# Feed-forward chunks 1 to 9 with the weight tile as stationary operand and the rows' two parts side by side

## The reference, cut to what matters

```python
def swiglu(h, w_gate, w_up, w_down):
    return (jax.nn.silu(h @ w_gate) * (h @ w_up)) @ w_down
# h: (256, 1024) float32, an rms_norm of x; w_gate, w_up: (1024, 2816); w_down: (2816, 1024)
# rmsnorm(x, g) = x * rsqrt(mean(x * x) + eps) * g
```

## Time and profile before

| | |
|---|---|
| median of 3 runs | 1907.35 us |
| lowest, highest | 1907.06, 1907.66 us |
| span of the profiled execution (first to last instruction) | 1904.2 us |
| the profiled execution's own time | not given apart; the median is 3.15 us over the span |
| PE, PEld busy | 98%, 80% |
| DVE, ACT, POOL busy | 58%, 50%, 8% |
| DMA moved | 332.72 MB, 175 GB/s over the span |

### The profile page before, as it was taken

How to read it: one execution, slowest core, us unless ns; L and a number is a source line. 1 busy time by engine, 2 the same in 40 slices (tenths; PEclk the granted TensorE clock), 3 DMA queues, 4 the chain that set the end, 5 groups by cost and what they waited for, 6 DMA issues and landing times.

```text
span 1904.2 us, 26150 instructions
## 1 busy us (share of the span) xinstructions
PE 1868.7 (98%) x8988; PEld 1523.3 (80%) x8988; DVE 1107.1 (58%) x1365; ACT 958.9 (50%) x1277; POOL 150.4 (8%) x259
## 2 busy tenths in 40 slices
PE   8999999999999999999999999999999999999998
PEld 7777888887877888888788887788888888868887
DVE  6666565448676575446754456655465445575454
ACT  5664454445675464445544446644454444564443
POOL 5210010001300010000100012000011000100000
PEclk9999999999999999999999999999999999999999
DMA  6335565554524546565655554455565564526553
GB/s 225 123 119 184 179 217 190 178 183 151 166 90 166 205 164 204 193 198 177 201 190 178 179 202 141 143 195 179 182 219 170 184 198 169 195 90 197 178 178 107
DMA packets 204987, 332.72 MB, mean 175 GB/s; under 512 B 11360, under 2 KB 150240, under 8 KB 204896
## 3 DMA queue, kind: packets, MB, share of 16 engines
q1 hardware_dynamic: 200240, 319.08, 49.9%
q0 software_dynamic: 3120, 11.02, 1.7%
q10 hardware_dynamic: 1536, 1.47, 0.2%
HBM read 330.48 MB, written 1.05 MB: 174 GB/s over the span
## 4 chain that ended last, share of the span: by engine, by line
PE 88%; issue 4%; DVE 3%; ACT 3%; DMA 1%; POOL 0%; DVEq 0%; SPq 0%; POOLq 0%; ACTq 0%
PE ps L571 27%; PE ps L565 27%; PE ps L556 27%; PE ps L598 3%; ACT whi L1254 1%; PE ps L771 1%; PE ps L759 1%; PE ps L787 1%; ACT prob L1352 1%; DVE wlo L1738 1%; DMA raw<-w_in_dram 0%; DVE prob L1878 0%; DMA xs<-x_dram 0%; DVE prob L1851 0%; DVE act_lo L1744 0%
## 5 line engine op out<-in xcount | busy, mean ns | idle before, releaser
L1738 DVE TENSOR_TENSOR wlo<-raw,whi 128x2048 fp32r<-128x2048 f32 (+1 forms) x306 | 690.6, 2257 | 510.3 <-ACT whi L1254 509.8
L1254 ACT ACTIVATE whi<-raw 128x2048 fp32r<-128x2048 f32 (+1 forms) x306 | 576.9, 1885 | 422.4 <-PE ps L565 422.3
L571 PE MATMUL ps<-whi,act_hi 128*128 128x512 f32 (+2 forms) x1632 | 442.0, 392 | 5.1 <-issue 2.4
L556 PE MATMUL ps<-wlo,act_hi 128*128 128x512 f32 (+2 forms) x1632 | 438.7, 387 | 0.0
L565 PE MATMUL ps<-whi,act_lo 128*128 128x512 f32 (+2 forms) x1632 | 432.2, 386 | 1.5 <-DVE act_lo L1744 1.5
L565 PEld LDWEIGHTS ps<-whi,act_lo 128*128 128x128 f32 x1632 | 303.9, 188 | 64.4 <-DVE act_lo L1744 2.3
L556 PEld LDWEIGHTS ps<-wlo,act_hi 128*128 128x128 f32 x1632 | 302.2, 188 | 61.8 <-issue 1.1
L571 PEld LDWEIGHTS ps<-whi,act_hi 128*128 128x128 f32 x1632 | 297.5, 188 | 64.1 <-issue 2.8
L1299 ACT ACTIVATE hid<-ps,stat 128x256 f32<-128x256 f32 x132 | 62.6, 474 | 282.9 <-PE ps L598 197.4
L2320 POOL TENSOR_TENSOR stat<-stat,eps 128x1 f32<-128x1 f32 x43 | 22.4, 521 | 1471.4 <-ACT prob L1286 1471.1
L1791 DVE SCALAR_TENSOR_TENSOR hid<-ps,stat,hid 128x256 f32<-128x256 f32 x132 | 63.6, 482 | 123.7 <-ACT hid L1299 123.7
(11 more groups left out here) (217 smaller groups left out, 1611.5 us busy)
## 6 DMA issues: line engine op xcount, KB each, us to landing
raw<-ffn_w_gate_dram SPq DMA_DIRECT2D x88, 512.0 KB, 4.0
raw<-ffn_w_up_dram SPq DMA_DIRECT2D x88, 512.0 KB, 5.0
raw<-ffn_w_down_dram SPq DMA_DIRECT2D x88, 512.0 KB, 3.9
raw<-w_in_dram SPq DMA_DIRECT2D x64, 512.0 KB, 4.4
raw<-w_ffn_gate_dram SPq DMA_DIRECT2D x44, 512.0 KB, 4.0
raw<-w_ffn_up_dram SPq DMA_DIRECT2D x44, 512.0 KB, 5.0
raw<-w_ffn_down_dram SPq DMA_DIRECT2D x44, 512.0 KB, 3.9
raw<-a_w_qkv_dram SPq DMA_DIRECT2D x24, 512.0 KB, 4.5
```

What stands on the lines that cost most here:

```text
L556: last = nc.tensor.matmul(o, hi, a, start=False, stop=last_pass and stop and i == len(parts) - 1)
L571: nc.tensor.matmul(o, hi, a, start=start and i == 0, stop=False)
L1254: nc.scalar.activation(whi[:, u % SLOTS, 0:words], raw[:, u % SLOTS, 0:words], ACT.Copy)\
L1738: nc.vector.tensor_tensor(wlo[:, u % SLOTS, 0:words], raw[:, u % SLOTS, 0:words], whi[:, u % SLOTS, 0:words].bitcast(F32), ALU.subtract)\
```

## The change

Chunks 1 to 9 compute gate and up transposed. For each 128 hidden columns (`j`) and each of gate and up (`g`) the weight tile is stationary and the rows stream: the high part of the weights over both halves of a new buffer `both`, which holds the rows' high and low parts side by side (512 columns), and the low part of the weights over the rows' high part (256 columns). One bank holds 256 columns of the first kind and 256 of high by low; ACT reads the low half out, DVE adds the other to it. The hidden result has hidden columns on the partitions, as `down` wants it, and isn't transposed. Gate and up of a chunk take banks 0 to 3. The norm scale now runs along the free axis: per feed-forward, a matrix of ones times a diagonal of the scales spreads it over the partitions (`spread_scale`), and DVE multiplies gate by it. The scale of up is left out of all chunks and applied to the down product at the end (`fold`). Chunks 0 and 10 keep their form; chunk 0's transposes go to banks 4 and 6, within half 0 of chunk 1. SP's program isn't changed; POOL gets one memset.

```diff
+        both = sb("act", [P, DT, 2, S], F32R)
+        act_hi, act_lo = both[:, :, 0, :], both[:, :, 1, :]
...
 PE:
+                def spread_scale(t):
+                    pe.wait_ge(sem("spread"), w.at("spread", nth * T + t + 1))
+                    nc.tensor.matmul(ps[:, 5 + 2 * t, 0:P], ones[:, :], diagonal[:, t, :],
+                                     start=True, stop=True).then_inc(sem("turn_done"), 1)
+                def columns(u, half, gu, first=False):
+                    unit_there(u)
+                    at = (slice(None), u % SLOTS, slice(None))
+                    vh, vl = (b[at].rearrange("p (k g n) -> p k g n", k=4, g=2) for b in (whi, wlo))
+                    for g in (1, 0) if first else (0, 1):
+                        for j in range(CH // P):
+                            if half == 0 and first and g == 0:
+                                if j == 0:
+                                    down_banks_there()
+                                turn_inner(gu - 2, tn, (j,), 4 + 2 * j)
+                                if j == 1:
+                                    for t in range(T):
+                                        spread_scale(t)
+                            elif half == 0 and j == 0 and not first:
+                                free_before("gu", gu + g)
+                            bank = ps[:, 2 * g + j, :]
+                            cols = slice(j * P, (j + 1) * P)
+                            for k in range(4):
+                                kt = 4 * half + k
+                                nc.tensor.matmul(bank[:, :], vh[:, k, g, cols], both[:, kt, :, :],
+                                                 start=half == 0 and k == 0, stop=False)
+                                last = nc.tensor.matmul(bank[:, 0:S], vl[:, k, g, cols], act_hi[:, kt, :],
+                                                        start=False, stop=half == 1 and k == 3)
+                        if half == 1:
+                            last.then_inc(sem("gu_done"), 1)
+                    if half == 0:
+                        last.then_inc(sem("used"), 1)
...
-                chunk(u + 2, gu + 2, tn, True)
-                with pe.Fori(0, NCH - 3) as i:
+                columns(u + 2, 0, gu + 2, True)
+                columns(u + 3, 1, gu + 2)
+                down(u + 4, 0)
+                with pe.Fori(0, COLUMNS - 1) as i:
                     w.chunk = i
-                    chunk(u + 5, gu + 4, tn + 2, False)
+                    columns(u + 5, 0, gu + 4)
+                    columns(u + 6, 1, gu + 4)
+                    down(u + 7, 1)
...
-                turn_hidden(gu - T, tn - T)
                 tile = gate_up(u, gu)
                 tile(0)
                 tile(1, (0,))
-                down(u + 2, tn - T, tiles=(0,))
-                turn_hidden(gu, tn, tiles=(0,))
+                down(u + 2, NCH - 2, tiles=(0,))
+                turn_inner(gu, late, tiles=(0,))
...
 ACT:
-                chunk(gu + 2, tn)
-                with act.Fori(0, NCH - 3) as i:
+                for t in range(T):
+                    turned_hi(tn + t, hid_hi[:, :, t * P:(t + 1) * P], CH // P, 4 + 2 * t)
+                for t in range(T):
+                    turned_copy(tn + T + t, scale_row[:, t * P:(t + 1) * P].unsqueeze(1), 1, bank=5 + 2 * t)
+                with act.Fori(0, COLUMNS) as i:
                     w.chunk = i
-                    chunk(gu + 4, tn + 2)
+                    split(1)
+                    inner_there(0)
+                    low_half(3, hid, 0)
+                    columns_silu(1)
+                    low_half(4, up_sum, 1)
+                    split(1)
+                    name, k = w.end_of(done[0] - SLOTS)
+                    act.wait_ge(sem(name), w.at(name, k))
+                    columns_hi(2)
+                    split(1)
...
-                hidden_hi(tn - T)
-                silu(gu, 0, tn - T)
+                inner_there(COLUMNS)
+                silu(gu, 0)
                 split(1)
...
 DVE:
+                def spread_scale(t):
+                    inverse_there(norm + t)
+                    nc.vector.tensor_scalar(fold[:, t:t + 1], scale_of(w, norm + t), share, None, ALU.mult)
+                    nc.vector.tensor_scalar(diagonal[:, t, :], ident[:, :], scale_of(w, norm + t), None, ALU.mult)\
+                        .then_inc(sem("spread"), 1)
+                def add_low(n, dst, g):
+                    dve.wait_ge(sem("low_half"), w.at("low_half", nth * 2 * COLUMNS + n))
+                    nc.vector.tensor_tensor(dst[:, :, :], ps[:, 2 * g:2 * g + 2, 0:S], dst[:, :, :], ALU.add)\
+                        .then_inc(sem("gu_read_v"), 1)
+                    dve.wait_ge(sem("gu_read_v"), w.at("gu_read_v", gu + T + n))
+                def columns():
+                    add_low(1, hid, 0)
+                    rows = scale_row.unsqueeze(1).to_broadcast([P, CH // P, S])
+                    nc.vector.tensor_tensor(hid[:, :, :], hid[:, :, :], rows, ALU.mult).then_inc(sem("times"), 1)
+                    add_low(2, up_sum, 1)
+                    silu_there(T + 1)
+                    nc.vector.tensor_tensor(hid[:, :, :], up_sum[:, :, :], hid[:, :, :], ALU.mult)\
+                        .then_inc(sem("times"), 1)
...
+                spread_scale(0)
+                times_up(0, 1)
+                split(1)
+                spread_scale(1)
+                times_up(1, 2)
+                split(1)
+                for t in range(T):
+                    turned_part(tn + t, t, hid_lo, hid_hi, 4 + 2 * t)
+                _, name, k = w.read("turn", tn + 2 * T - 1)
+                dve.wait_ge(sem(name), w.at(name, k))
+                split(1)
+                with dve.Fori(0, COLUMNS) as i:
+                    w.chunk = i
+                    columns()
                     split(1)
+                    columns_lo()
                     split(2)
...
-                hidden_lo(tn - T)
-                times_up(gu, 0)
-                split(1)
-                hidden_lo(tn, (0,), tail[:, 1], tail[:, 0])
-                times_up(gu, 1)
+                times_up(0, T + COLUMNS + 1)
+                turned_part(tn, 0, tail[:, 1], tail[:, 0])
+                times_up(1, T + COLUMNS + 2)
                 if first is not None:
                     first()
                 if then is None:
                     split(1)
-                hidden_lo(tn, (1,), tail[:, 1], tail[:, 0])
+                turned_part(tn + 1, 1, tail[:, 1], tail[:, 0])
...
-            def gained_half(n, g, hf, t):
+            def gained_half(n, g, hf, t, norm):
...
-                nc.vector.tensor_tensor(ht[:, t, :], half_bank(hf, 2), gains[:, g % 2, :], ALU.mult)\
-                    .then_inc(sem("half_read_v"), 1)
+                nc.vector.scalar_tensor_tensor(ht[:, t, :], half_bank(hf, 2), scale_of(w, norm), gains[:, g % 2, :],
+                                               ALU.mult, ALU.mult).then_inc(sem("half_read_v"), 1)
```

More of the change, by code:

```diff
@@ L127 @@
     half_hi=3 * FGROUPS, mirror_hi=FGROUPS, mirror_lo=FGROUPS, turn_hi=TURN_HI1.count("1"), pair_hi=H1,
-    squared=14, inverse=14, gain_in=48, aux_in=32, silu=2 * NCH,
+    squared=14, inverse=14, gain_in=48, aux_in=32, silu=2 * T + COLUMNS,
+    inner_hi=COLUMNS, inner_lo=COLUMNS, times=2 * COLUMNS, low_half=2 * COLUMNS, spread=T,
     h_ready=6, c_ready=2, x_ready=6, e_ready=2, merged=2,
@@ L276, in two_blocks @@
         ident = sb("ident", [P, P])
+        ones = sb("ones", [P, P])
+        fold = sb("fold", [P, T])
         mask = sb("mask", [P, T, S])
@@ L693, in down_by_columns, with down @@
                                 False, True).then_inc(done, 1)
-                def down(u, tn, tiles=range(T), start=False, stop=False, between=None):
+                def down(u, c, tiles=range(T), between=None):
                     unit_there(u)
+                    start, stop = c == 0, c == NCH - 1
                     hi, lo = (tail[:, 0], tail[:, 1]) if stop else (hid_hi, hid_lo)
                     vh, vl = u_view(whi, u, 2, D), u_view(wlo, u, 2, D)
+                    if not start and not stop:
+                        inner_there(c)
                     for t in tiles:
                         if start:
-                            free_before("half", hf + t)
-                            if w.layer is not None:
-                                was_read("half", hf - 1)
-                        was_read("turn", tn + t)
+                            was_read("turn", tn + t)
+                            was_read("turn", tn + T + t)
+                        if stop:
+                            was_read("turn", tn + 2 * T + t)
                         outs = [ps[:, 4 + 2 * t + n, :] for n in range(2)]
@@ L714, in down @@
                         last.then_inc(sem("used"), 1)
-                def chunk(u, gu, tn, start):
-                    tile = gate_up(u, gu)
-                    tile(0)
-                    turn_hidden(gu - T, tn)
-                    tile(1)
```

(17 more changed lines are left out.)

162 lines of the change are left out of this document (89 added, 73 removed).

## The result

The changed kernel takes 1926.26 us (median of 4 runs, 1925.17 to 1932.06) against 1907.2 for the kernel before (median of 4): ratio 1.0108, 95% interval 1.0096 to 1.0119. It is slower by 19 us, where no change was forecast, and outside the range of 1891 to 1915. The profiled execution took 1925.17 us, its span is 1923.5, 19.3 over the span of before. (Every timed execution takes 1.7 us more than its own span. The 3.15 us that the forecast added set the span of one execution of the kernel before beside the times of others, which were 1.4 us longer.)

A forecast was written before the change was run, and what follows sets the result against it. The loop was taken as bound by TensorE alone. Terms -25.9 + 8.0 + 3.0 + 13.7 - 0.5 = -1.7 gave span 1902.5, median 1905.7 us, under the 0.2% that can be told; range 1891 to 1915.

The forecast's parts named there:

- Edit 1: Chunks 1 to 9 lose the four transposes of the hidden tile: 54 x 0.48 = -25.9 us.
- Edit 2: Gate and up with weights stationary, 32 short products replacing 16 long: +0.147 us a chunk, +8.0 us over 54 chunks.
- Edit 3: Spreading the norm scale over partitions by fp32 products in each feed-forward: 0.5 us, six times, +3.0 us.
- a few ns each: In the loop, what the neighbours of the quad behind the transposes lose, booked within the transposes' 0.48 us a chunk.
- 258-column runs: Nearest products in the earlier trace, 119 ns each with a new stationary; used to price the 256-column products at 118.
- The room of 9 ns under a short product: In gate and up, a weight load needs 109 ns, as between transposes, so 118 ns hides it with 9 to spare.
- short products cost more than 118: Rival for gate and up: fixed cost per short product, 1.73 us for each ns; 1928 at 131 ns; chance 0.10.
- Edit 4: ScalarE's and VectorE's chain for gate and up in the steady loop: over 5 us of slack, so 0.
- the rival with 0.09: Helpers are late in the loop: one eviction of 0.6 us a chunk showing is +32, 1938; chance 0.09.
- Edit 5: At each tail, VectorE's split of unit 32 precedes the multiply, so TensorE waits 2.28 us; six times, +13.7 us.
- Its rival of 0.17: No wait at the tail: the multiply isn't held, 13.7 goes, sum -15.4, 1892; chance 0.17.
- Edit 6: Third feed-forward's start: chunk 1's up half first removes a 1.8 us wait, tile 1 is late; net -0.5 us.

The follow-up runs named there:

- e2_grouped: As e1_tail, but per bank and half the four 512-column products come first, then the four of 256; median 1904.86 us, ratio 0.9991 to the kernel before.
- e7_all_short: As e1_tail, but in 7 of 8 contraction tiles the 512-column product is made as two of 256 columns; 1917.93 us in one execution.
- e1_tail: The changed kernel with VectorE's third split moved from the end of the loop's body to its head; median 1910.38 us, ratio 1.0016 to the kernel before.
- e5_narrow_long: As e1_tail, but in 7 of 8 contraction tiles the 512-column product has 64 of its 128 weight columns as stationary; 1888.58 us in one execution.
- e9_long_112: As e5_narrow_long, but with 112 of 128 weight columns in the long products' stationary; 1898.56 us in one execution.
- e3_right: As e1_tail, but the 256-column products add to the right half of the bank instead of the left; 1909.5 us in one execution.

## Why the prediction was wrong, point by point

**Edit 1**, the transposes: 48 products of hid are left in place of 264, six times eight, and chunk 10's group gave 0.42 us a feed-forward (14.08 to 13.66) where 0.48 was summed. Right.

**Edit 2** is the step that failed: "+0.147 a chunk", from "Two columns less give 118". The short product's own distance was right, 117 ns. What was wrong was to leave the long one at 226.8 beside it: it measured 236 on the mean. In the loop, chunks 2 to 9, the edit cost 16.79 - 16.80 + 0.48 = 0.47 us a chunk, 48 times 22.4 us where 7.1 was summed, so 15.3 us were missed and the gain of edit 1 in the loop was eaten nearly whole. That alone took the result out of the range: 1926.3 less 15.3 is 1911. In chunk 1 it cost about what was forecast (edit 3, below). The runs show that the excess goes with the width of the stationary operand and with how closely short and long products alternate. The sign of it stood in the trace of before, in the stretch of the earlier trace rows. The nine products that follow the first one behind the transposes start 235, 234, 235, 225, 230, 236, 229, 232 and 231 ns apart, nearly what long products show behind four short ones in e2_grouped. I booked that as "a few ns each", the price of a transpose; it was what a run of short streams leaves to the long products behind it. (Most of the 0.11 us by which the quad at 301.40 is longer is something else: its first start is recorded 0.03 us after the last transpose, where a transpose's distance is 0.109.) And the 258-column runs were priced by their own distances, never by what followed them.

The room of 9 ns under a short product rested on the transposes, and their loads aren't like the others: this row of the kernel before has 139 ns for one, where the earlier trace rows has 188.

```profile
L598 PEld LDWEIGHTS ps<-ident,hid 128*128 128x128 f32 x264 | 33.1, 139 | 9.3
```

The rule of the Trainium skill, TensorE: Matmul & The Clock Gate, LDWEIGHTS, gives 107 ns for 128 columns, and I had found the transposes' 109 to agree. Read as I read it, that a load is hidden once the product over it takes longer, it would give no excess under a product that takes 113; e7_all_short shows 119.7 for load and product together, and where that reading and the run differ the run decides.

The rival nearest to this stood in the list as "short products cost more than 118", with 0.10, at a price for each short product of 1.73 us a ns: right in its place, in its sign and nearly in its size, since 353 ns a pair is as if the short one cost 126; by its own formula 8 ns over 118 give 13.8 us, where 15.3 were missed. That its 1928 for 131 ns lies near the measured 1926 is luck: the distance behind it wasn't 131, and the clock and the open rest made up the difference. (The top of the range, said to stand for 124 ns, is by the same formula 123.4.) The rival got too little because I asked for it in the wrong column, the short product's distance.

**Edit 3**: four instructions of 112 ns (L700 in the trace of e1_tail), 0.45 us. Chunk 1 in the fourth feed-forward went from 11.37 us (1231.67 to down's start at 1243.04) to 12.06:

```profile
1234.78 0.39 PE L725 MATMUL ps<-act,whi 128*128 128x512 f32 x1
...
1239.45 0.61 PE L700 MATMUL ps<-q,ones 128*128 128x128 f32 x4
...
1246.84 1.09 PE L584 MATMUL ps<-whi,hid_hi 128*128 128x512 f32 x4
```

That is +0.69, by the forecast's steps 0.147 + 0.5, less than 0.05 apart. Behind the fp32 products that spread the statistics the same pairs of e1_tail run at 347 ns (230 + 117) in the fourth feed-forward's chunk 1, not at 353. Why two patterns hold for one sequence of instructions isn't known.

**Edit 4**, the helpers' chain costed at nothing: right. The list of waits has no wait of TensorE for it; the rival with 0.09 fell.

**Edit 5**, the tail: 2.28 us forecast, 2.2 found, six times 13.3; e1_tail gave it back by the one split. Its rival of 0.17 fell. Not priced was the clock: the forecast named a fall below full speed as something that would make it wrong, and put no number on a wait of 2 us for it. It cost 1.6 us in two of six tails of the profiled execution, 3.3 us.

**Edit 6**: the third feed-forward's start is 0.14 us shorter where the other five are 0.87 to 1.45 longer, so about 1 us less than its like; -0.5 was forecast on top of the rest. The forecast took 1.8 us of waiting off and put 1.3 back for tile 1. In the traces 1.67 goes; tile 1 costs 0.28, and 0.39 is for the low part of the weights at chunk 1's start, which no term named.

**What stays open.** Of the 5.6 us between the feed-forwards chunk 1 makes 6 x 0.69 = 4.1, and the third's start takes 0.9 off; 2.4 are left. There TensorE's products fall behind those of before in steps of about 0.08 us, in code that the change left alone. Nothing was run on that. Nor is it settled by what a wide stationary operand costs the mixed products, load, array columns or output rows, why a long stream doesn't cover the short product's part of it, and why the excess stays with 112 columns once it is there; the runs fix the sizes only.

**Together**, in us: -23.0 (edit 1, 48 x 0.48) - 2.5 (chunk 10's groups) + 22.4 (edit 2 in the loop) + 4.1 (chunk 1, edits 2 and 3) - 0.9 (edit 6) + 13.3 (edit 5) + 3.3 (the clock) + 2.4 (open) = 19.1, the sum of the table's differences; the spans differ by 19.3.

## What to carry to other kernels

When a change replaces long streams by short ones at the same number of columns, price the products beside them too: read a mixed stretch of the trace, from one long product over the short ones to the end of the next long run, not the distance of the short ones alone. Group equal products, so that few short streams meet long ones. And when a loop's body is rearranged, write down which unit its last split is at the last iteration, and what stands behind it on that engine: here the place of one split cost 16.6 of the 19.3 us, with the clock's falls behind its waits.

## What the runs showed of the hardware that was not expected

- A product of 512 fp32r columns starts 226.7 ns before the next when its neighbours are long; one of 256 takes 113.3 with a 64-column load under it (e5_narrow_long), 119.7 in a run with 128-column loads (e7_all_short).
- Alternating, with 128-column loads, a pair takes 353 ns in a pattern of three (233 + 117, 241 + 120, 236 + 113), where the two alone would make 346; with 64 columns in the load under the short stream, 340; with 112, 340 until the first 128-column load and 350 from there on (e9_long_112).
- The excess outlasts the short products: down's first ten products behind them stand 224 to 241 ns apart before they settle at 227 (e1_tail), and its first quad lasts 1.11 us in place of 1.07. Behind the four transposes of the kernel before, the long products show nearly the same distances.
- A recorded load of 64, 112 and 128 fp32r columns takes 134, 175 and 188 ns (e5_narrow_long, e9_long_112), one of 128 columns ahead of a transpose 139 (the kernel before).
- The same wait of 2 us at the same place was followed by the lower clock level in two of the six tails of one execution, and not in the other four. At the seam of the two layers a wait of 2.11 us was followed by it (e5_narrow_long) and one of 2.64 us was not (e3_right).
- The kernel before has falls too, though its trace shows none: of its 19 executions beside e1_tail those with a mean granted clock of 0.999 took 1905.5 to 1906.3 us, those with 0.998 took 1907.1 to 1907.8.
- The same sequence of pairs runs at 347 ns in one place (chunk 1 of the fourth feed-forward, behind the fp32 products) and at 353 in the loop.
